# The first product of some units is taken in two halves of 64 rows

## The reference

```
mod_l = split(silu(c) @ w_mod + b_mod, 6);  hl = modulate(rms_norm(x, norm1_g), mod_l[0], mod_l[1])
zl = hl @ w_in + b_in                        # and the keys and values of the context from hc @ w_in
x  = x + mod_l[2] * ((g_conv * y_conv + g_sgu * y_sgu + g_att * y_att) @ w_o + b_o)
x  = x + mod_l[5] * (square(relu(modulate(rms_norm(x, norm2_g), ...) @ w_ff1 + b_ff1)) @ w_ff2 + b_ff2)
h  = [meta, rms_norm(x, final_g)]
h  = h + rms_norm(diff_attention(rms_norm(h)));  h = h + rms_norm(pool_mixer(rms_norm(h)));  return h[16:]
```

## Time and profile before

| | |
|---|---|
| median of 3 runs | 2723.61 us (2723.15 to 2725.39) |
| profiled execution | 2728.85 us, its span 2726.8 us |
| TensorE busy | 2666.2 us of the span, 21400 matmuls |
| VectorE, ScalarE, GpSimd busy | 1907.9, 1275.3, 152.3 us |
| HBM read | 533.57 MB, 196 GB/s over the span |
| granted TensorE clock, mean | 0.992 |

### The profile page before, as it was taken

The page is one execution under the profiler, slowest core; times in us unless marked ns, Lnnn a source line. Parts: engine busy times, 40 slices in busy tenths (PEclk is TensorE's granted clock), DMA queues, the critical chain, the costliest instruction groups (busy, mean ns, idle before and its releaser), DMA issues.

```text
span 2726.8 us, 51256 instructions
## 1 busy us (share of the span) xinstructions
PE 2666.2 (98%) x21400; PEld 2546.1 (93%) x21400; DVE 1907.9 (70%) x2865; ACT 1275.3 (47%) x1852; POOL 152.3 (6%) x162
## 2 busy tenths in 40 slices
PE   7999999999999999999999999999999999999998
PEld 4599977899999999989999999999999999989997
DVE  6766789889897788897555555577666665478564
ACT  5522344455446445554443544564444444554453
POOL 0000011100014000100000000030000000100000
PEclk9999999999999999999999999999999999999999
DMA  8766765465556788777555655654434444535553
GB/s 309 288 227 230 233 189 172 144 203 183 186 184 190 241 283 280 253 259 256 195 193 194 195 193 196 198 194 152 158 127 160 148 153 142 178 122 190 185 193 131
DMA packets 163989, 539.00 MB, mean 198 GB/s; under 512 B 31024, under 2 KB 35120, under 8 KB 163632
## 3 DMA queue, kind: packets, MB, share of 16 engines
q1 hardware_dynamic: 163760, 535.73, 59.0%
HBM read 533.57 MB, written 2.10 MB: 196 GB/s over the span
## 4 chain that ended last, share of the span: by engine, by line
PE 88%; DVE 7%; DMA 2%; ACT 1%; issue 1%; SPq 1%; DVEq 0%; POOL 0%; ACTq 0%
PE ps L575 26%; PE ps L580 26%; PE ps L577 26%; DVE lo L1713 2%; DMA raw<-in_w_ff 1%; PE ps L791 1%; PE ps L810 1%; PE ps L738 1%; PE ps L726 1%; PE ps L799 1%; DMA raw<-in_w_mod 1%; DVE row L2310 1%; PE ps L971 0%; ACT hi L1090 0%; PE ps L993 0%
## 5 line engine op out<-in xcount | busy, mean ns | idle before, releaser
L1090 ACT ACTIVATE hi<-raw 128x1024 fp32r<-128x1024 f32 x856 | 900.7, 1057 | 878.5 <-PE ps L580 458.6
L1713 DVE TENSOR_TENSOR lo<-raw,hi 128x1024 fp32r<-128x1024 f32 x856 | 1039.8, 1227 | 213.2 <-ACT hi L1090 211.8
L580 PE MATMUL ps<-AH,lo 128*128 128x256 f32 (+2 forms) x3504 | 992.7, 283 | 14.2 <-DVE lo L1713 14.2
L575 PE MATMUL ps<-AH,hi 128*128 128x256 f32 (+2 forms) x3504 | 1002.5, 286 | 2.7 <-DVE AL L2127 2.7
L577 PE MATMUL ps<-AL,hi 128*128 128x256 f32 (+2 forms) x3504 | 992.2, 283 | 0.0
L575 PEld LDWEIGHTS ps<-AH,hi 128*128 128x128 f32 x3504 | 662.4, 189 | 32.0 <-issue 29.9
L580 PEld LDWEIGHTS ps<-AH,lo 128*128 128x128 f32 x3504 | 662.7, 189 | 17.8 <-DVE lo L1713 17.8
L577 PEld LDWEIGHTS ps<-AL,hi 128*128 128x128 f32 x3504 | 662.7, 189 | 0.9
L580 PE MATMUL ps<-YH,lo 128*128 128x256 f32 (+1 forms) x1512 | 420.9, 278 | 0.9 <-DVE lo L1713 0.8
L575 PE MATMUL ps<-YH,hi 128*128 128x256 f32 (+1 forms) x1512 | 421.1, 279 | 0.0
L577 PE MATMUL ps<-YL,hi 128*128 128x256 f32 (+1 forms) x1512 | 421.0, 278 | 0.0
(11 more groups left out here) (287 smaller groups left out, 2948.6 us busy)
## 6 DMA issues: line engine op xcount, KB each, us to landing
raw<-in_w_ff SPq DMA_DIRECT2D x256, 512.0 KB, 4.2
raw<-in_w_in SPq DMA_DIRECT2D x208, 512.0 KB, 4.2
raw<-in_w_mod SPq DMA_DIRECT2D x192, 512.0 KB, 4.9
raw<-in_w_ain SPq DMA_DIRECT2D x128, 512.0 KB, 3.7
raw<-in_w_pin SPq DMA_DIRECT2D x64, 512.0 KB, 3.5
raw<-in_w_o SPq DMA_DIRECT2D x32, 512.0 KB, 4.7
raw<-in_w_aout SPq DMA_DIRECT2D x32, 512.0 KB, 3.5
raw<-in_w_pout SPq DMA_DIRECT2D x32, 512.0 KB, 4.0
```

The lines of the kernel that those rows point to most:

```text
L575: e.matmul(b.ap[:, o], hi[:, k, :], xh, start=start and k + i == 0, stop=False, skip_group_check=many)
L580: mm = e.matmul(b.ap[:, o], los[j % NSPLIT][:, k, :], xh, start=False, stop=stop and k == KU - 1, skip_group_check=many)
L1090: e.activation(his[u % NSPLIT][:, :, :], raws[raw_at[i]][:, :].rearrange("p (k m) -> p k m", k=KU), ACT.Copy).then_inc(s_hi, 1)
L1713: e.tensor_tensor(los[u % NSPLIT][:, :, :], raws[raw_at[i]][:, :].rearrange("p (k m) -> p k m", k=KU), his[u % NSPLIT][:, :, :].bitcast(F3 ...
```

## The change

A flag `broken` is set by three events: a `mean` over T = 256 tokens (a mean over another number clears it), the transposes of a `mod_turn`, and a tile of `gemm` that has `ready`. The next call of `unit` reads and clears it. If it was set, the unit's first product (L575 at k = 0, of the first part) is taken for rows 0 to 63 alone, and the product for rows 64 to 127 comes at the end of the unit, into the same part of the bank. The last half waits on a new semaphore that the first half raises. The unit's `s_unit` is raised by the last half.

```diff
                 j = unit_at
+                apart, broken = broken, False
...
                     for i, (xh, xl, o) in enumerate(parts(k0 + k)):
-                        e.matmul(b.ap[:, o], hi[:, k, :], xh, start=start and k + i == 0, stop=False,
-                                 skip_group_check=many)
+                        if apart and k + i == 0:
+                            e.matmul(b.ap[:, o], hi[0:64, k, :], xh[0:64, :], start=start, stop=False,
+                                     skip_group_check=many).then_inc(s_half, 1)
+                        else:
+                            e.matmul(b.ap[:, o], hi[:, k, :], xh, start=start and k + i == 0, stop=False,
+                                     skip_group_check=many)
...
-                                      stop=stop and k == KU - 1, skip_group_check=many)
+                                      stop=stop and k == KU - 1 and not apart, skip_group_check=many)
+                if apart:
+                    halves_at += 1
+                    e.wait_ge(s_half, halves_at)
+                    xh, xl, o = parts(k0)[0]
+                    mm = e.matmul(b.ap[:, o], hi[64:128, 0, :], xh[64:128, :], start=False, stop=stop,
+                                  skip_group_check=many)
                 mm.then_inc(s_unit, 1)
...
             def gemm(parts, free, n=2, ready=None):
+                if ready is not None:
+                    broken = True
...
             def mean(key, n, total=ssum, last=None):
+                broken = n == T
...
             def mod_turn(nb):
                 mm.then_inc(s_modt, 1)
+                broken = True
```

More of the change, by code:

```diff
@@ L398, in build @@
         s_dve, s_act = sem("s_dve_chain"), sem("s_act_chain")
+        s_half = sem("s_half")
         s_hi, s_lo, s_unit, s_mod, s_modt, s_modv = (
@@ L552, in _ @@
             s0, s1, tb, xb = Bank(S0), Bank(S1), Bank(TB), Bank(XB)
-            unit_at, tile_at = -1, 0
+            unit_at, tile_at, broken, halves_at = -1, 0, False, 0
             def opened(b):
@@ L560, in unit @@
             def unit(b, k0, parts, start, stop, ready=None):
-                nonlocal unit_at
+                nonlocal unit_at, broken, halves_at
                 unit_at += 1
                 j = unit_at
+                apart, broken = broken, False
                 for nb in mod_ends(j):
@@ L585, in gemm @@
             def gemm(parts, free, n=2, ready=None):
-                nonlocal tile_at
+                nonlocal tile_at, broken
                 b = opened(bank[tile_at % 4])
@@ L638, in mean @@
             def mean(key, n, total=ssum, last=None):
+                nonlocal broken
                 opened(xb)
```

## The result

The changed kernel takes 2773.77 us (median of 4, 2769.69 to 2776.4) against 2723.47 (median of 4, 2723.15 to 2725.39): ratio 1.0182, interval 1.0164 to 1.02. It is 50 us slower, where 2725 was forecast with a range up to 2738.

What follows compares the result with a forecast made beforehand. TensorE's own pace was taken to bound the kernel, its 256-column stream running at 113.35 or 117.8 ns. Marked units +17.6, covered ones +0.1, faster stretches -16.4 made +1.3 us: 2725 us, range 2717 to 2738.

Steps and rivals of the forecast that it cites:

- The count and the price of the halves: 28 marked units, each with a 64-row first and last product; 0.93 us for one paying in full.
- The sum: Whole kernel: +17.6 for units on the path, +0.1 for covered ones, -16.4 for faster stretches, +1.3 us; 68%.
- the 19 units: Marked units that pay on the path: sixteen in full, 14.9 us, and three behind L791 at 0.53, 1.6 us.
- the rival without emptying: At the halves: loads go in beside the product before, a marked unit costs only 0.113 us; 2709.6 us; 9%.
- a unit behind products of another row count starts in the fast rhythm: Assumption for units behind 64-row or four-row products: they start at 113 ns a product, not 118.
- 33 of 33: Units fast behind another row count: 32 behind L791's 64-row scores, one behind four-row products at 143.9; otherwise about one in two.
- The sign that the prediction named for being wrong: In the changed trace: steps of 113 around the halves, or 118 behind any last half.
- The term of -16.4 us: Slow stretches behind marked units, 215.65 to 1079.56 us, turn fast at 4.44 ns a product, 7.5 us of it at 640.05.
- fast already, pay and gain nothing: Marked units at 188, 244.8, 841.0, 991.6, 1035.6, 1043.8 and 1255.4 open fast stretches: they pay and gain nothing.
- the half doesn't set the rhythm: Rival: row change is another draw; unit behind 1255.4 slow costs 23.1 us, about 2748, else 2733; 14%, half each.
- New draws, zero within 1 us: Stretches behind unmarked transposes (v_turn, sgu_turn) are drawn anew, half slow as now: zero, within 1 us.
- Faster products running into waits: Rival: a wait for DVE's `lo` in a faster stretch redraws the rhythm, up to 7.5 us back at 640; 2732; 9%.

Runs made afterwards that it cites:

- exchanged: Changed kernel with the two halves exchanged: rows 64 to 127 first in a marked unit, rows 0 to 63 last; 2727.01 us, once more 2730.52 us.
- the two mended kernels: An extra whole-row product of 384 columns, result unused, in 14 places of the kernel before: 2719.16 us; the same products in the changed kernel: 2736.87 us.
- the map: Kernel before with one extra unused step behind each of 64 units of its long stretch, other steps in a second kernel; 2754.87 and 2764.75 us.
- the kernel with 14: Kernel before with an extra unused 384-column product in the first unit behind each of 14 interruptions between 188 and 1256 us; 2719.16 us, ratio 0.9966.
- the map's second kernel: Kernel before with 64 other extra unused steps in the long stretch, pairs of halves among them, and 50 in units of 272 columns; 2764.75 us.

## Why the prediction was wrong

- The count and the price of the halves were right. There are 28 at each end, 202 to 211 ns ahead of a half inside a stream or behind transposes and 309 to 311 behind it, then 220 to 227. The sum had 17.6 us; 16.7 of it lie before the units of 272 columns, where the rests give 14 to 16 (two profiles each: 1697.2 changed, 1699.2 exchanged, less 1682.9 before), and the medians of the two mended kernels differ by 17.7. Two of the prediction's figures are a little off and don't matter: 744 products at 4.44 ns are 3.3 us and not 3.5, and the 19 units have 70 emptyings of their own, 6.5 us, since the three behind L791 have two each. The emptying that the Trainium skill gives for a change of tiling mode (TensorEngine Tiling, Key Properties) shows at each half, at some 93 ns, so the rival without emptying is out. The other rule, which the prediction quotes from the Trainium skill at that rival (TensorE: Matmul & The Clock Gate, Part 3: a load overlaps with products in flight only when its row group differs), isn't what the stream here shows: at 113 ns a product it hides loads of all 128 rows beside products of all 128 rows. Where the rows do differ, the trace agrees: at 646.16 us a half directly behind one of the other rows starts 3 ns after it.
- The step that failed is "a unit behind products of another row count starts in the fast rhythm". Behind the last half of a unit that ran fast it started slow in 16 of 16 places. The 33 of 33 behind it weren't 33 trials: 32 of them were one kind of step behind one and the same rhythm, and such a step gives nearly always the same. For L791's successors even this ended: in the changed trace four of them were slow, and in the second profile of the kernel before itself the first of them, at 328.98 us and behind products at 118, was slow too. What I took for a property of the row count is one of the single step, with its rows, its columns and the rhythm ahead. The sign that the prediction named for being wrong, 118 behind a last half, is what the trace shows. Had the half of rows 0 to 63 been the last one, the assumption would have come out true at the last halves, by luck, and the time within 6 us of the forecast: 2727.01 and 2730.52.
- The term of -16.4 us came out as +29.1 (6546 more slow steps). A fast stream was taken for the end state; in fact each marked unit has two interruptions, and the second one turned what the first had mended. Of the stretches I called "fast already, pay and gain nothing", the one at 1255.4 lost 23.1 us.
- The rival "the half doesn't set the rhythm" had the place and the price (23.1 us at the unit behind 1255.4) at half of 14%. Its time, 2748, was still 26 too low: it kept the gain elsewhere, as if the long stretch could be lost alone, while one cause acts at all marks at once.
- "New draws, zero within 1 us" was too narrow for before itself: its two profiles differ by 1270 slow steps (5.6 us), and its timed runs span 43 us. The three runs that I had lay within 2.3 us and gave no hint of it.
- Faster products running into waits did not decide: VectorE's busy time hardly moved, and TensorE's idle time, span less busy, fell from 60.6 to 56.6 us.

## What to carry to other kernels

Where a stream has two rhythms at a granted clock of 1.00, read its steps' starts ahead of and behind every interruption, and tabulate what follows by the exact step and by the rhythm ahead; a count over one kind of step behind one rhythm is one observation, however many rows it has. A change that adds interruptions can cost its effect on the long stretches behind them, so price each by the length of what follows, all of them lost together. And time such a kernel in many runs: a narrow spread of three says little when one stretch of 5208 products can fall either way.

## What the runs showed of the hardware that was not expected

- The 256-column float32r stream runs at 113.35 or 117.8 ns a product, and exchanging which half of the rows a single product takes, with the same lengths in the trace, decided it in 50 of 50 and 27 of 27 places behind fast products. What in the engine holds the state stays open.
- Turning needs no change of rows: an extra whole-row product of 128, 160, 224 or 256 columns made a fast stream slow in 14 of 14 places of the map, at 175 to 233 ns from the regular start ahead to the next, one of 64, 96, 192, 384 or 512 left it fast in 10 of 10 (of 384, in other kernels, not always).
- An extra product of 384 columns costs 0.18 us (291 to 294 ns from the last regular start to the next in place of 113 to 118), and one such product ahead of a long stretch can be worth 7.4 us, as at 640 (the time from there to 841, first profile of before against the kernel with 14). In the second profile of before that stretch was fast without it.
- The stage at 2511 us runs 768 products of 256 columns at 118.9 ns in all profiles, and the ones right behind them (from 2602.7 us in the kernel before) at 113.3; products of 272 columns kept 125.2 whatever stood among them.
- Two halves of different rows that follow each other directly, into different banks and without a wait between them, cost no more than one: they start 3 to 4 ns apart, and whole start to whole start takes 519 to 525 ns where a single half takes 514 to 521 (8 pairs of the map's second kernel). In the kernel with both halves last they go into one bank with a semaphore wait between them, and start 438 ns apart; which of the two costs that was not tried. At the pair at 646.16 us of the changed kernel:

```profile
646.16 0.38 PE L592 MATMUL ps<-BH,hi 64*128 64x256 f32 x1
646.16 0.38 PE L578 MATMUL ps<-AH,hi 64*128 64x256 f32 x1
646.47 0.39 PE L583 MATMUL ps<-AL,hi 128*128 128x256 f32 x1
```
